# State-space heads of a diffusion backbone: whole exponents in one matmul, directions merged by a predicated copy, diagonal and skip term on GpSimd

## What is computed

```
cum  = cumsum(dt * a)                      # per direction and head
lmat = exp(where(s <= t, cum[t] - cum[s], -inf))
y_diag = ((C B^T) * lmat) @ (x * dt)       # inside a chunk
y_off  = exp(cum[t]) * C[t] . state        # from the chunks before
y_f, y_b = the scan forwards, and on the flipped tokens
y = (y_f + y_b + d_skip * x) * silu(z)     # then RMSNorm per group, @ w_out
```

## Time and profile before

| | us |
|---|---|
| median of three runs | 2128.65 (2124.43 to 2129.34) |
| profiled execution | 2124.56 |
| its span, first to last instruction | 2122.8 |
| PE busy | 2042.2 (96 %) |
| DVE busy | 1275.2 (60 %) |
| ACT busy | 862.9 (41 %) |
| POOL busy | 113.8 (5 %) |
| mean granted TensorE clock | 0.986 |

### The profile page before, as it was taken

How to read it: one execution, slowest core, us unless ns; L and a number is a source line. 1 busy time by engine, 2 the same in 40 slices (tenths; PEclk the granted TensorE clock), 3 DMA queues, 4 the chain that set the end, 5 groups by cost and what they waited for, 6 DMA issues and landing times.

```text
span 2122.8 us, 33441 instructions
## 1 busy us (share of the span) xinstructions
PE 2042.2 (96%) x12674; PEld 1806.5 (85%) x12674; DVE 1275.2 (60%) x1958; ACT 862.9 (41%) x1392; POOL 113.8 (5%) x175
## 2 busy tenths in 40 slices
PE   5999999999999999999999999999998999999998
PEld 3899999998889999999998878777875787888887
DVE  6666555557465773764756867777777543333335
ACT  3544433435232341331433555748384335232232
POOL 1011010110001000000000100000000000000000
PEclk8999999999999999999999999999999999999999
DMA  8432223223322432433322221211216223333332
GB/s 284 156 90 63 88 81 90 88 63 120 119 81 84 135 119 80 137 97 97 100 84 72 73 68 40 80 49 54 84 49 237 60 80 87 92 99 99 95 93 90
DMA packets 297917, 204.68 MB, mean 96 GB/s; under 512 B 5397, under 2 KB 289422, under 8 KB 296014
## 3 DMA queue, kind: packets, MB, share of 16 engines
q1 hardware_dynamic: 294349, 180.04, 28.8%
q0 software_dynamic: 3456, 23.09, 3.0%
HBM read 189.47 MB, written 13.63 MB: 96 GB/s over the span
## 4 chain that ended last, share of the span: by engine, by line
PE 81%; DVE 8%; ACT 5%; issue 3%; DMA 1%; SPq 1%; ACTq 0%; POOL 0%; DVEq 0%; POOLq 0%
PE G L328 56%; PE G L1241 13%; ACT e L1998 1%; PE S L2136 1%; PE S L874 1%; DVE acc L2167 1%; PE S L2132 1%; PE S L845 1%; PE S L453 1%; DVE wlo L315 1%; ACT whi L311 1%; DVE hn L746 1%; DVE hlo L755 1%; PE G L437 1%; DMA ada<-in_ada_w_dram 1%
## 5 line engine op out<-in xcount | busy, mean ns | idle before, releaser
L328 PE MATMUL G<-hhi,whi 128*128 128x384 f32 (+2 forms) x1760 | 574.7, 377 | 28.8 <-DVE hlo L755 19.8
L315 DVE TENSOR_TENSOR wlo<-raw,whi 128x1024 fp32r<-128x1024 f32 (+2 forms) x213 | 248.0, 1165 | 473.6 <-ACT whi L311 472.9
L328 PE MATMUL G<-hhi,wlo 128*128 128x384 f32 (+2 forms) x1760 | 532.4, 353 | 0.0
L328 PE MATMUL G<-hlo,whi 128*128 128x384 f32 (+2 forms) x1760 | 531.8, 353 | 0.0
L311 ACT ACTIVATE whi<-raw 128x1024 fp32r<-128x1024 f32 (+2 forms) x213 | 215.9, 1014 | 721.5 <-PE G L328 587.5
L328 PEld LDWEIGHTS G<-hhi,whi 128*128 128x128 f32 x1760 | 319.9, 191 | 95.1 <-issue 40.6
L328 PEld LDWEIGHTS G<-hhi,wlo 128*128 128x128 f32 x1760 | 327.1, 190 | 20.1
L328 PEld LDWEIGHTS G<-hlo,whi 128*128 128x128 f32 x1760 | 327.8, 191 | 17.5
L328 PE MATMUL G<-mhi,whi 128*128 128x384 f32 (+2 forms) x544 | 163.6, 349 | 2.0 <-issue 0.9
L328 PE MATMUL G<-mlo,whi 128*128 128x384 f32 (+2 forms) x544 | 162.6, 347 | 0.0
L328 PE MATMUL G<-mhi,wlo 128*128 128x384 f32 (+2 forms) x544 | 162.6, 347 | 0.0
(11 more groups left out here) (356 smaller groups left out, 2996.0 us busy)
## 6 DMA issues: line engine op xcount, KB each, us to landing
raw<-in_ffn_w_in_dram SPq DMA_DIRECT2D x52, 512.0 KB, 3.9
raw<-in_ssm_w_in_dram SPq DMA_DIRECT2D x41, 512.0 KB, 4.0
raw<-in_hg_w_in_dram SPq DMA_DIRECT2D x40, 512.0 KB, 4.0
adaw<-in_ada_w_dram SPq DMA_DIRECT2D x20, 1024.0 KB, 5.6
...
```

What stands on the lines that cost most here:

```text
L315: dve.tensor_tensor(wlo[pn.slot][:, 0:kt, :], raw[pn.slot][:, 0:kt, :], f32(whi[pn.slot][:, 0:kt, :]), ALU.subtract).then_inc(s["lo"], 1)
L328: ins = pe.matmul(G[:, tl.slot, g0:g0 + n], w[pn.slot][:, k, :], r[:, k_base + k, t0:t0 + n], start=(first and k == 0 and i == 0), stop=(l ...
```

## The change

- The exponent of a head is complete after one float32r matmul per direction: 40 rows contract the log decay of t (`cuts`, rows of `hrow`, against constant rows of ones and zeros in `hsel`) and the shift of s, log dt minus the cumulated decay (`shifts`, rows of `hsel`, against constant rows in `hrow`). The bf16 mask matmuls go. The rows of a group are brought by small DMAs from DRAM copies of `cuts` and `shifts` (`head_rows`, GpSimd's queue), 8 per group; the constant rows are made once by GpSimd.
- The directions share one tile: ScalarE copies the forward exponent to SBUF (`head_start`), VectorE overwrites the part above the diagonal with the backward exponent by a predicated copy (`head_select`), ScalarE takes one exponential of 512 columns without bias, in place (`head_decays`), VectorE multiplies with C B^T (`head_weights`). The next `heads_seg` waits for the predicated copy and no longer for the exponential.
- The diagonal of the backward direction is missing in that tile. It and the skip term are one factor per token and head, made by GpSimd (`own_tokens`): ten small instructions, one product of 2048 columns with x, two additions of 1024 columns into `ytm`. `head_out` of head 0 waits for these and moves from the end of j = 3 to the start of j = 4; the outputs of the other even heads move likewise. The skip activations on ScalarE and the additions into `yb` on VectorE go.

```diff
-            def pair_decays(hh):
-
-                r = hh % 2
+            def head_start(hh):
                 act.wait_ge(s["sm"], HPG * q + hh + 1)
                 if hh >= 2:
                     act.wait_ge(s["yd"], HPG * q + hh - 1)
-                for d in (0, 1):
-                    for b in range(LBLK):
-                        ins = act.activation(block(m[f"e{d}{r}"][:, :], b), block(S[:, d, :], b), ACT.Exp,
-                                             bias=m["shiftT"][:, b, bass.ds(q * HPG + (d * NH + hh), 1)])
-                ins.then_inc(s["em"], 1)
+                act.activation(m[f"e{hh % 2}"][:, :], S[:, 0, :], ACT.Copy).then_inc(s["ec"], 1)
+            def head_decays(hh):
+                act.wait_ge(s["sl"], HPG * q + hh + 1)
+                e = m[f"e{hh % 2}"][:, :]
+                act.activation(e, e, ACT.Exp).then_inc(s["em"], 1)
             for j in range(len(PANELS)):
                 if ss is None and j in SO_SPLITS:
...
                         if q is not None and 3 <= j < 7:
-                            pair_decays(2 * (j - 3))
-                        if q is not None and ci == 1:
-                            act.wait_ge(s["skip"], q * GT + GT)
+                            head_start(2 * (j - 3))
                         if ci:
                             convolved(ci - 1)
+                        if q is not None and 3 <= j < 7:
+                            head_decays(2 * (j - 3))
                         if ci or q is not None:
...
@@ -2034,15 +2044,12 @@
                     convolved(len(CONVS) - 1)
                 if q is None and j in DT_ACT:
                     next(dt)
-                if q is not None and j == 1:
-                    act.wait_ge(s["yout"], q * 32 + 16)
-                    for i_ in range(GT):
-                        act.activation(m["yb"][:, i_, :], m["xfm"][:, i_, 0:NLAT], ACT.Identity,
-                                       scale=m["dsk"][:, bass.ds(q * GT + i_, 1)]).then_inc(s["skip"], 1)
                 if q is not None and 3 <= j < 7:
                     if before is None:
-                        pair_decays(2 * (j - 3))
-                    pair_decays(2 * (j - 3) + 1)
+                        head_start(2 * (j - 3))
+                        head_decays(2 * (j - 3))
+                    head_start(2 * (j - 3) + 1)
+                    head_decays(2 * (j - 3) + 1)
                 if q is not None and j == 7:
                     for i_ in range(GT):
                         act.wait_ge(s["yz"], GT * q + i_ + 1)
...
+        def head_select(dve, q, hh):
+            dve.wait_ge(s["ec"], HPG * q + hh + 1)
+            dve.memset(m["carry"][:, :], 0.0)
+            dve.copy_predicated(by_block(m[f"e{hh % 2}"][:, :]), m["later"][:, :, :].to_broadcast([P, LBLK, P]),
+                                by_block(S[:, 1, :])).then_inc(s["sl"], 1)
         def head_weights(dve, q, hh):
-            r = hh % 2
             dve.wait_ge(s["em"], HPG * q + hh + 1)
-            e0, e1 = m[f"e0{r}"][:, :], m[f"e1{r}"][:, :]
-            dve.tensor_tensor(e0, e0, e1, ALU.add).then_inc(s["mm"], 1)
-            dve.wait_ge(s["mm"], 2 * (HPG * q + hh) + 1)
-            dve.tensor_tensor(e0, e0, m["cb"][:, :], ALU.mult).then_inc(s["mm"], 1)
+            e = m[f"e{hh % 2}"][:, :]
+            dve.tensor_tensor(e, e, m["cb"][:, :], ALU.mult).then_inc(s["mm"], 1)
         def head_out(dve, q, hh):
+            if hh == 0:
+                dve.wait_ge(s["owna"], 2 * q + 2)
             dve.wait_ge(s["yd"], HPG * q + hh + 1)
             yt = m["ytm"][:, :, hh * HP:(hh + 1) * HP]
             dve.tensor_tensor(yt, yt, S[:, 2 + hh % 2, 0:LBLK * HP].rearrange("p (b c) -> p b c", c=HP),
...
                     split_lo(dve, At(PAN_SO + SO_SPLITS[j]), KT)
-                if q is not None and j == 0:
-                    for part in (0, 2 * NH):
-                        for d in (0, 1):
-                            ins = dve.tensor_copy(m["sel"][part:part + 2 * NH, d * HPG:(d + 1) * HPG],
-                                                  ident[part:part + 2 * NH, bass.ds(q * HPG + (d * NH + part), HPG)])
-                    ins.then_inc(s["cbs"], 1)
+                h0 = 2 * (j - 3)
                 if q is not None and 3 <= j < 7:
-                    head_weights(dve, q, 2 * (j - 3))
                     if j > 3:
-                        head_out(dve, q, 2 * (j - 3) - 1)
+                        head_out(dve, q, h0 - 2)
+                    head_select(dve, q, h0)
+                    head_weights(dve, q, h0)
+                    if j > 3:
+                        head_out(dve, q, h0 - 1)
                 for u in range(4):
                     if q is not None and j < 3:
                         chain_vector(dve, q, 4 * j + u)
+                    if q is not None and 3 <= j < 7 and u == 3:
+                        head_select(dve, q, h0 + 1)
                     tap(u + 1)
                 if q is None:
                     for _ in range(DT_DVE.count(j)):
                         next(dt)
                 if q is not None and 3 <= j < 7:
-                    head_weights(dve, q, 2 * (j - 3) + 1)
-                    head_out(dve, q, 2 * (j - 3))
+                    head_weights(dve, q, h0 + 1)
                 if q is not None and j == 7:
                     if ss is None:
                         split_lo(dve, At(PAN_SO + SO_SPLITS[j]), KT)
+                    head_out(dve, q, HPG - 2)
                     head_out(dve, q, HPG - 1)
                     for i_ in range(GT):
                         yb = m["yb"][:, i_, :]
                         dve.wait_ge(s["ytt"], GT * q + i_ + 1)
-                        dve.tensor_tensor(yb, yb, S[:, i_, :], ALU.add).then_inc(s["ya"], 1)
-                    for i_ in range(GT):
-                        yb = m["yb"][:, i_, :]
...
+        def head_rows(pool, g):
+            hs = slice(g * HPG, (g + 1) * HPG)
+            for e in (0, 1):
+                for d in (0, 1):
+                    r = (2 * e + d) * HPG
+                    pool.dma_start(m["hrow"][r:r + HPG, :], cut_park[e, d, hs, :]).then_inc(s["hin"], 16)
+                    pool.dma_start(m["hsel"][HK + e * LBLK:HK + (e + 1) * LBLK, d * HPG:(d + 1) * HPG, :],
+                                   shift_park[e, d, hs, :].rearrange("h (b t) -> b h t", t=P)).then_inc(s["hin"], 16)
+        def own_tokens(pool, q):
+            def step(n, ins):
+                ins.then_inc(s["owns"], 1)
+                pool.wait_ge(s["owns"], 11 * q + n)
+            def heads(ap):
+                return ap.rearrange("p (b a) -> p b a", a=1).to_broadcast([P, LBLK, HPG])
+            pool.wait_ge(s["stc"], 6 * q + 2)
+            step(1, pool.tensor_tensor(by_block(m["own"][:, :]), by_block(m["cb"][:, :]),
+                                       ident[:, :].rearrange("p (a t) -> p a t", a=1).to_broadcast([P, LBLK, P]), ALU.mult))
+            half = P // 2
+            for n in range(7):
+                own = by_block(m["own"][:, :])
+                to = m["owncb"][:, :].rearrange("p (b a) -> p b a", a=1) if half == 1 else own[:, :, 0:half]
+                step(2 + n, pool.tensor_tensor(to, own[:, :, 0:half], own[:, :, half:2 * half], ALU.add))
+                half //= 2
+            step(9, pool.tensor_tensor(m["ownx"][:, :, :], m["dtT"][:, :, q * HPG:(q + 1) * HPG], heads(m["owncb"][:, :]),
+                                       ALU.mult))
+            step(10, pool.tensor_tensor(m["ownx"][:, :, :], m["ownx"][:, :, :],
+                                       m["dall"][:, q * HPG:(q + 1) * HPG].rearrange("p (a h) -> p a h", a=1)
+                                       .to_broadcast([P, LBLK, HPG]), ALU.add))
+            pool.wait_ge(s["stc"], 6 * q + 6)
+            pool.wait_ge(s["yout"], q * 32 + 16)
+            step(11, pool.tensor_tensor(m["xown"][:, :, :].rearrange("p b (h c) -> p (b h) c", c=HP),
+                                       m["xtm"][:, 0:LBLK, :].rearrange("p b (h c) -> p (b h) c", c=HP),
+                                       m["ownx"][:, :, :].rearrange("p b (h a) -> p (b h) a", a=1)
+                                       .to_broadcast([P, LBLK * HPG, HP]), ALU.mult))
+            pool.wait_ge(s["ymc"], 12 * q + 12)
+            for bs in (slice(0, 2), slice(2, 4)):
+                pool.tensor_tensor(m["ytm"][:, bs, :], m["ytm"][:, bs, :], m["xown"][:, bs, :], ALU.add)\
+                    .then_inc(s["owna"], 1)
         def heads_seg(pe, q, hh):
             if hh == 0:
                 for d in (0, 1):
                     pe.wait_ge(states_of[d], state(q, NBLK - 1))
-                pe.wait_ge(s["cbs"], q + 1)
+                pe.wait_ge(s["hcon"], 2)
+                pe.wait_ge(s["hin"], 128 * q + 128)
             else:
-                pe.wait_ge(s["em"], HPG * q + hh)
+                pe.wait_ge(s["sl"], HPG * q + hh)
             for d in (0, 1):
```

(42 more changed lines are left out.)

48 lines of the change are left out of this document (29 added, 19 removed).

## The result

The changed kernel's median is 2136.32 us (2130.13 to 2143.99), that of the kernel before, measured beside it on the same chip, 2124.88 us: a ratio of 1.0057 with a 95 % interval of 1.0043 to 1.0072. The change makes the kernel slower by about half a per cent. One further run took 2270.22 us at a granted clock of 0.843; runs disturbed in this way are left out of every comparison.

The account below looks back on a forecast made before the run. TensorE bounds the chain stretch, TensorE and ScalarE the heads' panels. Three bodies 7.8, last group 0.5 and start 2.6 gave +10.9 us on 2124.6, so 2135.5, and 2137 with 2 us added; range 2118 to 2153.

Parts of the forecast that it names:

- The ring: Loop-body heads: one panel's ScalarE-VectorE dependency cycle takes 12.2 us instead of 10.99 and sets all panels; +1.5 us per body.
- the walk from head to head: Loop-body heads: adding times from first exponent product to last output gives 46.4 us against 45.2.
- The additions: Loop bodies: GpSimd's two additions after the last chain step delay queued VectorE work; +1.1 us per body, bounds 0 and 4.8.
- VectorE's slack of 6 us: Loop-body chain stretch: spare VectorE time absorbs the 1.5 to 4 us lost to GpSimd's long multiplication.
- TensorE's saving: All four groups: dropping 64 mask matmuls frees 14.9 us, 3.7 per group, which reappears as waits in loop bodies.
- The hold: Last group's chain: GpSimd's long multiplication blocks VectorE for 4.3 us, +5 with its effect on two later steps.
- the second rival: Whole kernel: GpSimd gives way to VectorE or shares, so no full-length blocking; 2124 us, chance 0.22.
- no long hold: Title of the second rival: GpSimd does not block VectorE for whole instructions; 2124 us, chance 0.22.
- the low clock: Waits over a microsecond may lower TensorE's clock, 1.7 us per drop; part of a 2153 us rival, chance 0.16.
- The end: After the last heads: 2.4 us less VectorE work before the squares, then the rstd wait remains; -1.5 us.
- The start: Before the first panel: GpSimd's selector fill delays the weight split and TensorE; +2.6 us, bounds 0 and 4.
- TensorE-bound throughout: Whole kernel: the select always arrives in time, so 14.9 us are saved in full; 2109 us, chance 0.12.

Follow-up runs that it names:

- the early select and the pieces: Changed kernel with the odd head's select behind the first convolution tap, not the third, and GpSimd's long instructions cut into 512-column pieces: 2109.17 us, ratio 0.9939.
- three blocks: Changed kernel with three output-product blocks of the last pass moved from panel 8 to between the first two heads' exponents: 2126.88 us, ratio 1.0016.

## Why the prediction was right, and where it was not

The median came within 1 us of the 2137.0 on record, and the difference of the medians, 11.4 us, is near the 10.9 of the sum. The 2 us put on top, for a median above the profiled run, had no ground: over eight runs the median of the kernel before lies 0.3 us above its profiled run. The loop bodies carried the sum as forecast; the last pass did not, and its error was made up behind it.

*The ring: right.* ScalarE, panel j = 5 of the second body, kernel after, beside the earlier trace rows:

```profile
1444.95 1.04 ACT L316 ACTIVATE whi<-raw 128x1024 fp32r<-128x1024 f32 x1
...
1447.32 1.28 ACT L1996 ACT_TABLE_LOAD   x1
...
1449.57 1.28 ACT L2010 ACT_TABLE_LOAD   x1
...
1456.59 0.63 ACT L2010 ACTIVATE e<-e 128x512 f32<-128x512 f32 x1 [3.69 <-DVE e L2149]
1457.13 1.04 ACT L316 ACTIVATE whi<-raw 128x1024 fp32r<-128x1024 f32 x1
```

From copy to copy 12.18 us (forecast 12.2), both table loads still in it; before 10.99. The heads alone grew by 0.8 us, not the 1.5 that I took: the walk from head to head had given 1.2, and the 0.3 for the later split was not there. ScalarE waits for the select 15.5 us in five waits, about 3.1 a panel (3.5 forecast). The select took 0.72 us, the value scaled by columns from the earlier trace rows; the broadcast mask costs nothing that shows.

*The additions: right place, small size.* +1.4 us a body against 1.1. The two take 5.46 us and not 4.8: the first is as long as reckoned (2.34 against 2.4), the second is held up by VectorE. The multiplication I had let disappear in VectorE's slack of 6 us. Its cover held for TensorE in the chain stretch (busy 42.60 of 42.60), but the slack was VectorE's margin for the next stretch too, and 0.1 to 1.2 us of it were paid there. Ring +2.3, additions +4.2, multiplication +2.2 (with 0.3 of clock in it): 8.7 of the 9.1 us.

*TensorE's saving: the term that was mis-sized.* 64 x 0.233 = 14.9 us rests on the exponent products costing the same after as before. A head's matmuls of the kernel before and of the one after, last pass, both at full clock:

```profile
1632.39 0.49 PE L2326 MATMUL S<-cuts,sel 128*128 128x512 f32 x1
1632.72 0.39 PE L2328 MATMUL S<-neg,identb 128*128 128x512 bf16 x1
1632.76 0.58 PE L2326 MATMUL S<-cuts,sel 128*128 128x512 f32 x1
1633.18 0.39 PE L2328 MATMUL S<-neg,identb 128*128 128x512 bf16 x1
1633.22 0.58 PE L328 MATMUL G<-yhi,whi 128*128 128x512 f32 x1
```

```profile
1667.31 0.73 PE L2380 MATMUL S<-hrow,hsel 40*128 40x512 f32 x2
1667.97 0.50 PE L333 MATMUL G<-yhi,whi 128*128 128x512 f32 x1
```

Four took 0.83 us, two take 0.66: 0.17 us saved. In the loop bodies, where the exponents stood behind a block without a wait, the four took only 0.73:

```profile
1440.54 0.40 PE L2326 MATMUL S<-cuts,sel 128*128 128x512 f32 x1
...
1441.27 0.58 PE L328 MATMUL G<-hhi,whi 128*128 128x512 f32 x1
```

That leaves 0.07 there. The masks' own 0.47 is about right (two such matmuls cost 0.53 above), so each of the new exponent products takes 0.33 us where 0.233 was assumed. TensorE's busy time of a whole loop body, both at clock 1.00, says much the same: 108.6 us before and 107.3 with the early select and the pieces, 1.3 us instead of 3.7. In all that is at most some 5 us, not 14.9. It did not show in the sum, as TensorE was not what set the bodies: its waits in the heads stretch are 5.7 us (3.6 and 2.1) where I had said near 9, against 3.0 before. And it lifted the pace of the last heads to 3.14 us, where I had reckoned 2.8.

*The last pass.* The hold came as described. Timelines of GpSimd and VectorE of the kernel after:

```profile
1624.21 3.63 POOL L2361 TENSOR_TENSOR xown<-xtm,ownx 128x2048 f32<-128x2048 f32 x1
...
1624.54 3.85 DVE L2118 TENSOR_TENSOR st<-st,dec 128x512 f32<-128x512 f32 x1
1628.48 0.69 DVE L2132 TENSOR_TENSOR st<-st,S 128x512 f32<-128x512 f32 x1
```

An instruction of 0.68 us takes 3.85 and ends 0.55 us behind GpSimd's: +3.2 for VectorE (forecast 4.3, because the multiplication takes 3.63 us and not 4.7), +3.1 for the chain (forecast 5). This was the case on which the second rival hung, and with it falls "no long hold". The Trainium skill (SBUF — State Buffer, Who interferes with whom) has the two engines shut each other out for a whole instruction; at 3.6 us the trace agrees.

The heads were to gain 3 us and lost 7.1. That is the step that failed: the low clock, which I had priced at 1.7 us a drop and put into a rival only. Where it stays away they take 27.3 us with three blocks more in them, 1.9 less than before, near the forecast. So the drop is worth about 9 us, by the profiled heads (36.2 to 27.3, with 2.1 us more work in them) and by the medians (1.0057 to 1.0016). The "waits of over a microsecond" of that rival are no measure: the clock fell behind 0.56 us in one kernel and stayed up behind 2.26 in another. TensorE, kernel after, when the clock fell and when it was back:

```profile
1641.91 0.73 PE L2380 MATMUL S<-hrow,hsel 40*128 40x512 f32 x2 [2.27 <-DVE e L2149]
...
1647.32 1.22 PE L2380 MATMUL S<-hrow,hsel 40*128 40x512 f32 x2
...
1664.17 0.73 PE L2380 MATMUL S<-hrow,hsel 40*128 40x512 f32 x2
```

*The end.* From the last heads to rstd -3.0 against -1.5, and behind it -4.2 where I had nothing. The forecast 1.5 is there: from the end of the transposes to the sums of squares 6.4 us became 4.9, and TensorE's wait of 1.23 us for VectorE is gone. Nearly all the rest is clock that the kernel before had lost and the changed one kept. The 16 transposes took 3.63 us at a granted clock of 0.66, now 1.97. The first 30.6 us behind rstd ran at 0.94, now at 1.00, which is 1.8 us. And 72 us behind rstd the clock was low in both, but longer before, which is another 1.7 us (before, then after):

```profile
1741.00:1750.00 9.00, 7.48 (x40) 7.49 (x41) 6.39 (x16) 3.08 (x7) 0.69 (x1) 0.62 0.21 60
...
1757.65:1766.65 9.00, 8.66 (x57) 8.22 (x57) 7.12 (x18) 3.96 (x8) 0.70 (x1) 0.81 0.21 60
```

The remaining 0.7 us stay open. One profiled run of each kernel cannot tell whether these drops belong to the kernel before or to that run. The last of them cost 1.7 to 3.0 us in kernels made from the changed one that do the same work behind rstd.

*The start.* The selector's fill took 3.60 us and ended at 1186.1 (1186.5 forecast), and split and first product were held:

```profile
1182.50 3.60 POOL L2549 TENSOR_TENSOR hsel<-ident 32x2048 fp32r<-32x2048 f32 x1
...
1184.49 2.69 DVE L320 TENSOR_TENSOR wlo<-raw,whi 128x1024 fp32r<-128x1024 f32 x1 [2.23 <-ACT whi L316]
...
1187.24 0.62 PE L333 MATMUL G<-hhi,whi 128*128 128x384 f32 x2 [1.94 <-DVE wlo L320]
```

The wait grew from 0.48 to 1.94 us, and the product came 2.0 us later than before. At 1247 all of it was still there (transposes at 1245.63 and 1247.64), at 1263 only 0.4: in between the kernel before lost more clock than the changed one, 0.28 against 0.14 of 12 us, or 1.7 us (before, then after):

```profile
1244.00:1256.00 12.00, 10.45 (x59) 9.27 (x59) 3.92 (x4) 8.74 (x12) 0.00 (x0) 0.72 0.25 65
...
1244.00:1256.00 12.00, 10.44 (x64) 8.82 (x63) 5.63 (x6) 10.77 (x17) 2.60 (x5) 0.86 0.36 100
```

The forecast of the hold was better than the table's +0.4 makes it look.

So the number was good and half of its reasons with it; that the rest cancelled is luck. The bodies alone gave 9.1 us. The last pass, with what follows it, came to +3.0 against a forecast of +0.5, only because the low clock in the heads stood beside some 5 us that the profiled run of the kernel before had lost to its own clock at the end. Another 1.7 us of that kind hid the hold at the start. *TensorE-bound throughout* was the wrong case for this kernel. With the select early and the pieces the kernel does take that rival's 2109 us, but not for its reason: of the 3.6 us by which a body's heads are shorter than before (45.2 to 41.6), TensorE's work gave 1.4, and 2.2 are waits of the kernel before (3.0 us) that are down to 0.84.
